# Forty modulation slots: row tiles summed on VectorE, partitions added on TensorE

## What is computed

```python
def adaln(cond, w, b):
    return (jax.nn.silu(cond) @ w + b)[:, None, :]

def pre_norm(x, mod, j, g):
    return rmsnorm(x, g) * (1 + mod_chunk(mod, 3 * j + 1)) + mod_chunk(mod, 3 * j)

def post_residual(x, out, mod, j, g, w):
    return x + w * mod_chunk(mod, 3 * j + 2) * rmsnorm(out, g)

def swiglu(h, w_in, w_out):
    gate, up = jnp.split(h @ w_in, 2, axis=-1)
    return (jax.nn.silu(gate) * up) @ w_out
```

## Time and profile before

| | |
|---|---|
| median of three runs | 1664.52 us (1664.42 to 1666.88) |
| the profiled execution, its own time | 1668.12 us |
| its span, first to last instruction | 1665.5 us |
| TensorE busy | 1612.6 us, 97% |
| VectorE busy | 835.1 us, 50% |
| ScalarE busy | 694.1 us, 42% |
| DMA | 259.83 MB, mean 156 GB/s |
| mean granted TensorE clock | 0.992 |

### The profile page before, as it was taken

One profiled execution on the slowest core, in us unless ns is written; L12 is line 12 of the kernel. 1 busy time (PEld: TensorE's weight loads), 2 busy tenths in 40 slices (PEclk: granted clock), 3 DMA queues, 4 the chain that ended last, 5 costly groups with the idle time before them and its releaser, 6 DMA issues.

```text
span 1665.5 us, 27671 instructions
## 1 busy us (share of the span) xinstructions
PE 1612.6 (97%) x11325; PEld 1570.2 (94%) x11325; DVE 835.1 (50%) x1323; ACT 694.1 (42%) x1205; POOL 42.0 (3%) x46
## 2 busy tenths in 40 slices
PE   5999999999998999999999999999999999999997
PEld 4999999999887988999999999999999989999997
DVE  5544434463456988443434744443472876343333
ACT  3433333353453456333334633333363256333332
POOL 2000000001100000000000000000000000000000
PEclk8999999999999999999999999999999999999999
DMA  9733366667983126433343633336363465333311
GB/s 329 232 126 126 126 214 223 202 210 229 282 278 95 51 90 194 138 127 127 115 133 126 203 127 126 126 122 207 127 203 127 135 221 176 126 126 120 114 45 38
DMA packets 255663, 259.83 MB, mean 156 GB/s; under 512 B 6625, under 2 KB 253826, under 8 KB 255570
## 3 DMA queue, kind: packets, MB, share of 16 engines
q1 hardware_dynamic: 249664, 251.67, 46.8%
q10 hardware_dynamic: 4978, 4.41, 0.8%
q0 software_dynamic: 928, 2.44, 0.6%
HBM read 255.88 MB, written 2.62 MB: 155 GB/s over the span
## 4 chain that ended last, share of the span: by engine, by line
PE 88%; DVE 7%; issue 2%; ACT 1%; DMA 1%; SPq 1%; DVEq 0%; ACTq 0%
PE bank L406 25%; PE bank L407 25%; PE bank L408 25%; PE bank L1460 3%; PE bank L1504 1%; PE bank L427 1%; PE bank L429 1%; PE bank L428 1%; DVE X L1060 1%; DMA RAW<-in_mod_w 1%; SPq L484 1%; PE bank L1733 1%; DVE WL L373 1%; DVE HL L1025 1%; DVE SUMS L1316 1%
## 5 line engine op out<-in xcount | busy, mean ns | idle before, releaser
L373 DVE TENSOR_TENSOR WL<-RAW,WH 128x1024 fp32r<-128x1024 f32 (+1 forms) x335 | 401.1, 1199 | 693.4 <-ACT WH L359 692.9
L359 ACT ACTIVATE WH<-RAW 128x1024 fp32r<-128x1024 f32 (+1 forms) x344 | 358.0, 1045 | 651.8 <-PE bank L408 639.1
L406 PE MATMUL bank<-HH,WH 128*128 128x384 f32 x1664 | 562.4, 338 | 7.2 <-DVE WL L373 3.1
L407 PE MATMUL bank<-HL,WH 128*128 128x384 f32 x1664 | 559.9, 336 | 0.0
L408 PE MATMUL bank<-HH,WL 128*128 128x384 f32 x1664 | 559.8, 336 | 0.0
L406 PEld LDWEIGHTS bank<-HH,WH 128*128 128x128 f32 x1664 | 313.3, 188 | 10.3 <-DVE WL L373 3.7
L407 PEld LDWEIGHTS bank<-HL,WH 128*128 128x128 f32 x1664 | 313.4, 188 | 0.0
L408 PEld LDWEIGHTS bank<-HH,WL 128*128 128x128 f32 x1664 | 313.4, 188 | 0.0
L406 PE MATMUL bank<-AH,WH 128*128 128x384 f32 x704 | 237.3, 337 | 0.0
L407 PE MATMUL bank<-AL,WH 128*128 128x384 f32 x704 | 236.6, 336 | 0.0
L408 PE MATMUL bank<-AH,WL 128*128 128x384 f32 x704 | 236.6, 336 | 0.0
(11 more groups left out here) (225 smaller groups left out, 1406.3 us busy)
## 6 DMA issues: line engine op xcount, KB each, us to landing
RAW<-in_ffn_w_in SPq DMA_DIRECT2D x88, 1024.0 KB, 5.1
RAW<-in_mod_w SPq DMA_DIRECT2D x72, 1024.0 KB, 6.8
RAW<-in_ffn_w_out SPq DMA_DIRECT2D x32, 1024.0 KB, 5.3
RAW<-in_ab_w_in SPq DMA_DIRECT2D x16, 1024.0 KB, 8.4
RAW<-in_ffn_w_out SPq DMA_DIRECT2D x16, 768.0 KB, 4.7
RAW<-in_cv_w_in SPq DMA_DIRECT2D x12, 1024.0 KB, 6.6
RAW<-in_ab_w_out SPq DMA_DIRECT2D x4, 1024.0 KB, 8.6
RAW<-in_cv_w_out SPq DMA_DIRECT2D x4, 1024.0 KB, 5.2
```

The lines of the kernel that those rows point to most:

```text
L359: e.activation(WH[:, (2 * m + b) % 4, 0:nk, :], RAW[:, p, 0:nk, b * P:(b + 1) * P], ACT.Copy).then_inc(half_hi, 1)
L373: e.tensor_tensor(WL[:, k, 0:nk, :], RAW[:, p, 0:nk, b * P:(b + 1) * P], WH[:, k, 0:nk, :].bitcast(F32), ALU.subtract).then_inc(half_ready, 1)
L406: e.matmul(out, WH[:, k, kk, :], xh(kk), start=(first and kk == 0), stop=False)
L407: e.matmul(out, WH[:, k, kk, :], xl(kk), start=False, stop=False)
```

## The change

Ten of the 18 modulation groups (40 slots) leave `mod_pair`. They form three stretches inside feed-forward sub-layers: modA, 16 slots, in s = 0; modF, 12 slots, in s = 2; modG, 12 slots, in s = 3. The attention keeps one group (modC, in the projections); the five groups of the turnovers and mod0 stay. For each of the 40 slots VectorE sums over the eight row tiles, for each of the two condition vectors: 16 operations of 128 x 256, the first of each sum a product, the other seven multiply and add. TensorE then adds over the partitions: four matmuls whose weights are 128 x 128 of the sums and whose moving operand is one column of ones. Slots 0 to 9 are summed in pairs 2 to 20 and added behind the third half of the pair that follows; the rest in the second product, behind the first half of slot n + 2.

```diff
+SUMMED = {0: "modA", 2: "modF", 3: "modG"}
+SUMMED_OUT = (0, 1, 3, 4, 6, 7)
+SUMMED_IN = 10
+            def mod_sums(s, q, steps):
+                st, n0 = SUMMED[s], summed_before(s) + q
+                p, uses = ring_at(st, q)
+                a = partial(s, q)
+                if steps[0] == 0:
+                    dve.wait_ge(raw_landed[p], 16 * (uses + 1))
+                    if n0 >= 2:
+                        dve.wait_ge(mod_reduced, n0 - 1)
+                for kk in steps:
+                    for g in range(2):
+                        w, by = RAW[:, p, kk, :], COND[:, kk, g:g + 1]
+                        if kk == 0:
+                            x = dve.tensor_scalar(a[:, g, :], w, by, None, ALU.mult)
+                        else:
+                            dve.wait_ge(mod_step, 16 * n0 + 2 * kk + g - 1)
+                            x = dve.scalar_tensor_tensor(a[:, g, :], w, by, a[:, g, :], ALU.mult, ALU.add)
+                        x.then_inc(mod_step, 1)
```

In `pair` on VectorE, with `mods` standing for `mod_sums` of slot j / 2 - 1:

```diff
                     nxt[0][0]()
                     nxt[0][1]()
+                    mods(0, 1)
                     for b in range(2):
                         nxt[1][b]()
+                        mods(2 + 2 * b, 3 + 2 * b)
...
+                    mods(6, 7)
```

On TensorE:

```diff
-            def mod_group(st):
+            def mod_reduce(s, q):
+                n0, k = summed_before(s) + q, q // 2
...
+                a = partial(s, q)
+                pe.wait_ge(mod_step, 16 * n0 + 16)
+                for t in range(2):
+                    for g in range(2):
+                        at = 4 * (q % 2) + 2 * t + g
+                        mm = pe.matmul(sum_bank(k)[:, at:at + 1], a[:, g, t * P:(t + 1) * P], ONES[:, 0:1],
+                                       start=True, stop=True)
+                mm.then_inc(mod_reduced, 1)
...
                         pe_half(pe, st, 2 * j + 2 + b, hh, hl, 8, cols3(bank[2 + b]), True, True, i)
+                        if b == 0 and j >= 4 and s in SUMMED:
+                            mod_reduce(s, j // 2 - 2)
...
-                    elif 3 <= step < 22:
-                        if step == 3:
-                            pe.wait_ge(proj_out, 12)
-                        mod_pair("modC", 4 + 2 * ((step - 3) // 2))
-                    if step % 4 == 0 and step >= 8:
-                        mod_turn(g0 + 1 + (step - 8) // 4)
...
-                pe.wait_ge(mod_cols, g0 + 6)
...
-                pe.wait_ge(conv_step, 4 * 4 + 1)
-                mod_group("modI")
...
-                mod_turn(first_group("modI"))
```

More of the change, by code:

```diff
@@ L67, with summed_slots, summed_before, turned_before @@
 BETWEEN = ("modB", "modD", "modE", "modH", "modJ")
-MOD_GROUPS = {"mod0": 2, "modA": 1, "modK": 1, "modL": 1, "modB": 1, "modC": 6, "modD": 1, "modE": 1, "modG": 1,
-              "modH": 1, "modI": 1, "modJ": 1}
+MOD_GROUPS = {"mod0": 2, "modA": 4, "modB": 1, "modC": 1, "modD": 1, "modF": 3, "modE": 1, "modG": 3, "modH": 1,
+              "modJ": 1}
+SUMMED = {0: "modA", 2: "modF", 3: "modG"}
+SUMMED_OUT = (0, 1, 3, 4, 6, 7)
+SUMMED_IN = 10
+COLS_OUT = {1: 4, 3: 5, 6: 6, 9: 7}
+def summed_slots(s):
+    return 4 * MOD_GROUPS[SUMMED[s]] if s in SUMMED else 0
+def summed_before(s):
+    return sum(summed_slots(r) for r in range(s))
+def turned_before(g):
+    names = list(MOD_GROUPS)
+    return sum(1 for n in names if n not in SUMMED.values() for at in range(first_group(n), first_group(n) + MOD_GROUPS[n])
+               if at < g)
 def first_group(st):
@@ L138, in plan @@
         place[st, n] = len(freed)
-        if st.startswith("mod"):
+        if st in SUMMED.values():
+            summed += 1
+            freed.append(("sum", summed))
+        elif st.startswith("mod"):
             mod += 1
@@ L394, in ffn_pairs @@
             after_first()
[L395 to L398, removed]
+            for j in range(2, 22, 2):
+                body(0, j)
         def pe_half(e, st, jj, xh, xl, nk, out, first, last, i=0):
@@ L491, in wait_ring @@
                         sp.wait_ge(half_ready, 2 * count)
+                    elif kind == "sum":
+                        sp.wait_ge(mod_step, 16 * count)
                     else:
@@ L1137, in ffn @@
                         half()
-                    if n in groups_at:
-                        coefficients(groups_at[n])
+                    q = SUMMED_IN + SUMMED_OUT.index(n) if n in SUMMED_OUT else SUMMED_IN + 6
+                    if n in (4, 10) and (12 if n == 4 else 16) <= summed_slots(s):
+                        coefficients(first_group(SUMMED[s]) + (2 if n == 4 else 3))
+                    if q < summed_slots(s):
+                        mod_sums(s, q, range(KD))
                     if n % 3 == 2:
@@ L1233, in even @@
                         coefficients(g0)
-                    if step % 4 == 3 and step >= 11:
-                        coefficients(g0 + 1 + (step - 11) // 4)
                 assert ticks[0] == 18, ticks
```

145 lines of the change are left out of this document (78 added, 67 removed).

## The result

| | before | after |
|---|---|---|
| median of the runs | 1667.17 us (1664.42 to 1669.17, 7 runs) | 1671.53 us (1669.79 to 1671.77, 7 runs) |
| ratio, 95% interval | | 1.0024 (1.0015 to 1.0034) |
| profiled execution, its own time | 1668.12 us | 1669.79 us |
| its span | 1665.5 us | 1667.2 us |
| TensorE, VectorE, ScalarE busy | 97%, 50%, 42% | 96%, 64%, 41% |

The change makes the kernel slower by 0.24%, a little more than the 0.2% taken as the limit of what can be told. 1671.5 us lies inside the range (1657 to 1674), above the forecast's own (1663 to 1669), and "slower" had 0.40 against 0.44 for "the same". The times of each kernel fall in groups: two of the seven of the kernel before lie near 1664.5 and five from 1666.9 to 1669.2; three of the kernel after lie at 1669.8 to 1670.0 and four at 1671.5 to 1671.8.

The account below looks back on a forecast made before the run. TensorE, busy 97% of the span, was taken to bound the kernel. Reductions add 35.2 us and removed work saves 32.9, so +2.3 on 1664.5 gives 1666.8 us, range 1657 to 1674.

Parts of the forecast that it names:

- 40 reductions: TensorE's new matmuls adding over partitions: 0.88 us each, eight records and the switch, 35.2 us added.
- groups and turns in feed-forward parts: Removed from dense TensorE work: four groups at 3.83 us and four turns at 0.45 us, 17.1 us saved.
- attention, net: Ten pairs and five turns removed from attention save 21.2 us, 6.5 us return as waits: 14.7 us saved.
- s = 4: Group and turn removed before the second product: 1.1 of 4.3 us saved, since TensorE then waits for VectorE's low part.
- three odd steps: Attention steps 7, 13, 19: without the pair TensorE waits 0.5 to 0.7 us for scaled probabilities, 1.8 us together.
- gross 21.2 us: Attention's saving from removed pairs and turns if nothing else held TensorE, before waits are subtracted.
- rival D: TensorE's clock falls behind new waits, in s = 4 and at attention's two sigmoids, 2 us each: 1672.8 us; chance 0.10.
- rival C: VectorE is late in the second product of s = 0, beyond 6.8 us a slot: +5 us, 1671.8 us; chance 0.07.
- A: Nothing returns as waits: attention yields 21.2 us and s = 4 yields 4.3 us, so 1657.1 us; chance 0.11.
- B: Attention takes back 12.2 us instead of 6.5, 0.7 us in each of ten odd steps: 1672.5 us; chance 0.12.
- E: A one-column matmul costs its issue alone, 0.34 us a slot, 21.6 us less in all: 1645.2 us; chance 0.03.
- Writing the loop out: In the first product of s = 0 TensorE is busy throughout, loop turns included, so unrolling wins nothing.

Follow-up runs that it names:

- Experiments 1: Kernel after, each of the 40 reductions making one matmul instead of four, three quarters of the additions over partitions left out: 1645.16 us.
- 2: Kernel after, each of a reduction's four matmuls moving 64 columns of ones instead of one: 1670.71 us.
- Experiment 9: Strips version with modI back in s = 4, plus one old-way group back in attention (pairs behind steps 9 and 11), modF with two groups: 1659.79 us.
- Experiment 4: Kernel after with 96 unused small strip matmuls filling TensorE's 3.0 us wait in s = 4 before the second product: 1669.14 us.
- experiment 7: Kernel after with extra 128 x 128 VectorE products in each summed slot: 14 a slot 1688.45 us, six a slot 1671.75 us.
- e_modI_kept: Kernel after with old-way group modI (four slots) back in the wait of s = 4, modG with two groups instead of three: 1666.39 us.
- experiment 8: Kernel after with modI back in s = 4; its strips kernel also uses ones as weights and moves sums in four strips: 1660.89 us, again 1660.90 us.

## Why the prediction was right or wrong

The median came out 4.7 us above the 1666.8 of the prediction. Of that some 2.6 us are its base: it took 1664.52, of three runs of the kernel before, two of which lie in the lower group, and the median of seven is 1667.17. The other 2.1 us are the change: +4.4 by medians (+4.5 by the stages) for +2.3. By its own terms, the measured ones from the stages, with the clock as in both profiles of before:

| term | predicted | measured |
|---|---|---|
| 40 reductions | +35.2 | +36.4 (40 x 0.91; s = 2: 10.9 to 11.05 for 12) |
| groups and turns in feed-forward parts | -17.1 | -17.2 (three in s = 0: 13.05; one in s = 3: 4.1) |
| attention, net | -14.7 | -15.4 |
| s = 4 | -1.1 | +1.04 |
| s = 5 and the rest | 0 | -0.3 |
| sum | +2.3 | +4.5 |

The reduction's 0.91 is measured by itself in s = 2; the old groups are what is left in s = 0 and s = 3 when it is taken off. Two small misses, +1.2 in the reductions and -0.7 in the attention, partly cancel; that is luck.

**The reduction.** Right in kind and nearly in size: 0.80 us for eight records and 0.10 for the edges, not 0.88 in all. Experiments 1 and 2 show that it goes by the number of records and not by what moves, as worked out from the turns and the sums.

**The old slots in feed-forward parts.** Right: 4.28 us a group with its turn was predicted, 4.1 to 4.35 measured.

**The attention.** The waits that the pairs had covered do come back, in the place and by the engines named: ScalarE's copy behind its sigmoids, VectorE's scaling. They are 5.15 us against 6.5. I had three odd steps at 0.5 to 0.7; there were two at 0.50. By the prediction's gross 21.2 us that would give 16.05; the stage gives 15.4, and where the other 0.7 us are is open. Experiment 9 shows the cover from the other side: pairs put back there cost about half of themselves (2.0 of 4.2 us).

**s = 4: the step that failed.** "Only 0.7 us are won, and 0.45 for the turn" left out what a wait does to the clock, which I had as rival D at 2 us for this place, with a chance of 0.10. Experiment 4 shows it: 1.58 us. And the turn was hardly on the path: in the kernel after TensorE has a wait of 1.27 us for ScalarE at 1346.38, where before the turn stood with 0.93 us of wait behind it, so of its 0.45 us 0.34 came back as wait. With the clock held up s = 4 is 0.54 us shorter than before, about the 0.7 alone. I had looked for cover behind the fifth turn of the attention and not behind this one.

**VectorE.** Right: 64%, 0.40 from start to start, no wait for `mod_step`. The point for rival C was put at 6.8 us a slot; measured, it lies between 7.2 and 8.7, in the second product of s = 0 and once in three slots, as the sum over threes said. At 7.2 that sum gives 3 x 0.9 = 2.7 us of delay and no wait was seen, so by it the lead that TensorE can eat was at least 2.7 us and not 2. The Trainium skill's rule that the next operation waits for an empty pipe ("VectorE: DVE Perf Modes", The DRAIN you can't avoid) gave me 7.5 us a slot; four multiply-adds of 479 ns take 1.67 us and not 1.92. The prediction left out that the same section makes an exception of an operation that isn't held, which starts earlier, so the rows and the section need not differ.

**The other rivals.** A (nothing given back): out, all its waits are there. B (7.5 us back in attention): out, 5.15. C: out, TensorE never waits for the sums in the kernel after, and by experiment 7 not at 7.2 us a slot either. E: out, by experiment 1; what spoke for it is answered in experiment 2. D came true in s = 4; in attention it comes and goes by execution (experiment 4 at 435 and 475 us).

**Writing the loop out** was put at nothing, and that is right: s = 5 is 0.3 us shorter than before in all seven profiles without modI, but 0.06 to 0.08 us longer in the four that have modI back, and the loop is written out in these too. What became shorter lies in the turnover behind s = 4: from its first sum to the second turn of `STAT` are 6.01 us before and in e_modI_kept, 5.65 in the kernel after. Why is open.

**What stays open.** Why the kernel before has two groups of times 2 to 4 us apart. Falls of the clock in attention differ from execution to execution and cost 1 to 1.6 us each, but the filler in step 2 did not remove the groups, and there is no profile of the lower group. So it can't be said which stage is shorter in it. The mean granted clock of each timed run points at the clock somewhere: over the sessions of the experiments the 26 runs of before in the lower group had 0.993 or 0.994, the 47 in the upper 0.992 in the mean (0.989 to 0.994). The difference of 0.002 is 3 us of 1665, as large as the gap between the groups.

## What to carry to other kernels

Work that fills a wait is cheaper than its busy time says, and moving it costs twice: once in the new place, and once because an idle TensorE may come back at a lower clock (0.67 over 5 us in s = 4). Price each place by itself: here 4.1 to 4.35 us a group in dense parts, about 2.0 in the attention's waits, half a microsecond in s = 4 (with the fall of the clock counted, the group there saves 1.0 us), against a new price of 3.6. And price a short visit of another kind of matmul by its edges (0.1 us for each slow step) and by its records; with full weights the moving side was free up to 64 columns.

## What the runs showed of the hardware

- A small fp32 matmul with 128 x 128 weights is two records of 0.10 to 0.11 us, the same with 1 and 64 moving columns.
- Eight strip records are 0.24 us inside a run of them, and a visit of eight between other matmuls is 0.55 us.
- One wait of TensorE of 1.16 us was followed by a clock of 0.66 to 0.78 over 5 us in some executions and of 1.00 in others: 0.66 in the kernel of experiment 9 and 1.00 in both profiles of experiment 8 with strips, whose programs on TensorE are alike up to there. With the gap filled by strip matmuls it was 1.00, in one execution. Behind the wait of 3 us it fell in all six profiles that have it, and not with the filler or with modI there; the matmuls behind it started 0.32 us apart instead of 0.17 for 3.7 us.
